# A pair's eight sums in two groups of four on four banks, and the row transposes behind the activations'

## The reference

```
for i in range(DEPTH):                       # 2 layers
    h = h + (gated_deltanet(...) if i == 0 else dilated_attention(...))
    h = h + hierarchical_moe(rms_norm(h), ...)
    h = h + per_layer_embedding(h, p[i], ...)
# hierarchical_moe: of 32 experts, each row goes to the best two of its best group
hdn = silu(xb @ w1[e]) * (xb @ w3[e])        # w1, w3: 1024 x 512
y   = hdn @ w2[e]                            # w2: 512 x 1024
out = zeros.at[row_tok].add(y * row_w)       # weighted rows summed back to their tokens
```

## Time and profile before

| | us |
|---|---|
| median of 3 runs | 1733.32 (1730.41 to 1734.15) |
| span of the profiled execution | 1731.8 |
| TensorE (PE) busy | 1677.2, 97% |
| VectorE (DVE) busy | 710.0, 41% |
| ScalarE (ACT) busy | 452.4, 26% |
| up products, L2158, 2040 matmuls | 460.7 |
| down products, L2195, 1008 matmuls | 223.4 |
| spread, L2145, 240 high and 240 low matmuls | 106.7 and 95.2 |
| adds, L2094, 240 | 154.0 |

### The profile page before, as it was taken

One profiled execution on the slowest core, in us unless ns is written; L12 is line 12 of the kernel. 1 busy time (PEld: TensorE's weight loads), 2 busy tenths in 40 slices (PEclk: granted clock), 3 DMA queues, 4 the chain that ended last, 5 costly groups with the idle time before them and its releaser, 6 DMA issues. The chain is left out here.

```text
span 1731.8 us, 20065 instructions
## 1 busy us (share of the span) xinstructions
PE 1677.2 (97%) x7380; PEld 806.9 (47%) x7380; DVE 710.0 (41%) x1514; ACT 452.4 (26%) x693; POOL 140.0 (8%) x192
## 2 busy tenths in 40 slices
PE   7999999998999999998999999998999999999898
PEld 4555566644334344343355564554343443434343
DVE  4778455515334343342333113365243443434241
ACT  5767233313010010101034716653110101101020
POOL 0026620001000000000000101100000000000000
PEclk9999999999999999999999999999999999999999
DMA  8121432286999999999991010058999999999950
GB/s 289 52 73 38 130 86 73 99 349 227 408 427 427 426 427 425 427 428 427 422 345 49 1 74 32 1 199 320 366 427 427 427 425 427 427 427 428 427 195 38
DMA packets 89355, 481.59 MB, mean 278 GB/s; under 512 B 22721, under 2 KB 39873, under 8 KB 62657
## 3 DMA queue, kind: packets, MB, share of 16 engines
q1 hardware_dynamic: 84672, 472.16, 67.3%
q0 software_dynamic: 4608, 8.40, 1.3%
HBM read 476.86 MB, written 12.06 MB: 282 GB/s over the span
## 5 line engine op out<-in xcount | busy, mean ns | idle before, releaser
L2158 PE MATMUL bank<-ring,xT 128*64 128x512 f32 x2040 | 460.7, 598 | 17.3 <-DMA ring<-in_w 16.4
L2094 DVE TENSOR_TENSOR H<-H,bank 128x512 f32<-128x512 f32 x240 | 154.0, 683 | 295.8 <-PE bank L2145 295.8
L2158 PEld LDWEIGHTS bank<-ring,xT 128*64 128x64 f32 x2040 | 140.1, 137 | 280.9 <-issue 264.8
L2195 PE MATMUL bank<-ring,sg 128*64 128x512 f32 x1008 | 223.4, 595 | 1.7 <-issue 1.2
L2195 PEld LDWEIGHTS bank<-ring,sg 128*64 128x64 f32 x1008 | 70.4, 137 | 131.0 <-issue 125.1
L705 PE MATMUL bank<-ring,ring 128*128 128x512 f32 x256 | 130.0, 604 | 0.0
L690 PE MATMUL bank<-ring,ring 128*128 128x512 f32 x256 | 112.9, 593 | 0.0
L2651 PE MATMUL bank<-ring,ring 128*128 128x512 f32 x256 | 110.5, 592 | 0.0
L2248 ACT ACTIVATE sg<-bank 128x512 f32<-128x512 f32 x32 | 19.2, 599 | 348.1 <-PE bank L2169 348.1
L2145 PE MATMUL bank<-high,Sb 128*128 128x512 f32 x240 | 106.7, 445 | 0.0
L2084 DVE SCALAR_TENSOR_TENSOR low<-bank,weight_now,high 128x512 fp32r<-128x512 f32 x60 | 45.1, 751 | 135.5 <-ACT high L2259 132.5
(11 more groups left out here) (346 smaller groups left out, 1985.1 us busy)
## 6 DMA issues: line engine op xcount, KB each, us to landing
ring<-in_w SPq DMA_DIRECT2D x178, 2048.0 KB, 28.6
ring<-in_w_heads SPq DMA_DIRECT2D x16, 1024.0 KB, 5.4
ring<-in_w SPq DMA_DIRECT2D x10, 1024.0 KB, 9.3
ring<-in_w SPq DMA_DIRECT2D x18, 512.0 KB, 7.4
ring<-in_w_ple_gate SPq DMA_DIRECT2D x4, 2048.0 KB, 28.7
ring<-in_w SPq DMA_DIRECT2D x4, 1536.0 KB, 8.2
ring<-in_w_kv SPq DMA_DIRECT2D x3, 2048.0 KB, 20.4
ring<-in_b_w_q SPq DMA_DIRECT2D x3, 2048.0 KB, 19.4
```

The costliest lines, as they stand in the source:

```text
L2094: dve.tensor_tensor(out, out, k.bank[6 + j % 2][:, :], ALU.add).then_inc(s.added, 1)
L2158: last = pe.matmul(out[e * SLOTS:(e + 1) * SLOTS, :], k.xT[:, at, e * SLOTS:(e + 1) * SLOTS], rows, start=(at == 0), stop=(at == DC - 1))
L2195: last = pe.matmul(k.bank[2 + n][e * SLOTS:(e + 1) * SLOTS, :], k.hT[:, c, e * SLOTS:(e + 1) * SLOTS], w[:, e, :], start=(c == 0), stop=(c ...
```

## The change

The sums of a pair are done in two groups. The first four stand where the first two stood, after the second half of `w1`; the second four after the second half of `w3`. They use banks 6, 7, 2, 3 and then 2, 3, 6, 7. Banks 2 and 3 are those of the down product, so the first group waits for both halves of the split, and the down product waits until the sums on banks 2 and 3 have been added. The activations' transposes come right behind the second group, and both halves of the next rows' transposes come behind these. VectorE adds the second four sums in one row, and evacuates both halves of the rows after them. The loop for more than 64 rows keeps banks 6 and 7.

```diff
+def spread_bank(j):
+    return (6, 7, 2, 3, 2, 3, 6, 7)[j]
-def add_results(dve, k, s, i, js):
+def add_results(dve, k, s, i, js, alone=False):
...
-        dve.tensor_tensor(out, out, k.bank[6 + j % 2][:, :], ALU.add).then_inc(s.added, 1)
+        bank = 6 + j % 2 if alone else spread_bank(j)
+        dve.tensor_tensor(out, out, k.bank[bank][:, :], ALU.add).then_inc(s.added, 1)
...
+def spread_matmuls(pe, k, s, j, bank):
+    n, t = j // NT, j % NT
+    for m, part in enumerate(parts_of(k, n)):
+        last = pe.matmul(bank[:, :], k.Sb[:, t * P:(t + 1) * P], part, start=(m == 0), stop=(m == 1))
+    last.then_inc(s.spread, 1)
+def spread_first(pe, k, s, i):
+    pe.wait_ge(s.Sb, i + 1)
+    pe.wait_ge(s.low, 2 * i + 2)
+    wait(pe, s.added, 8 * i)
+    for j in range(NT):
+        spread_matmuls(pe, k, s, j, k.bank[spread_bank(j)])
+def spread_second(pe, k, s, i):
+    for j in range(NT, 2 * NT):
+        if j < NT + 2:
+            pe.wait_ge(s.added, 8 * i + j - 1)
+        spread_matmuls(pe, k, s, j, k.bank[spread_bank(j)])
...
 def expert_down(pe, k, s, i, memory, arrived, alone=False, first=False):
     pe.wait_ge(s.hT, i + 1)
-    if not alone:
+    if not (alone or first):
         wait(pe, s.low, 2 * i)
+        pe.wait_ge(s.added, 8 * i - 2)
...
     pe.wait_ge(s.low, 2 * (PAIRS - 1))
+    pe.wait_ge(s.added, 8 * (PAIRS - 1) - 2)
...
-            spread(pe, k, s, i - 1, (0, 1))
+            spread_first(pe, k, s, i - 1)
         expert_up(pe, k, 1, 0, memory, k.bank[1], s.half2, arrived)
-        if not first:
-            spread(pe, k, s, i - 1, (2, 3))
         expert_up(pe, k, 1, 1, memory, k.bank[1], s.h3, arrived, apart=k.early_quarter if first else None)
         if not first:
-            spread(pe, k, s, i - 1, (4, 5))
+            spread_second(pe, k, s, i - 1)
+        expert_turn(pe, k, s, i)
         if not last:
             turn_rows(pe, k, s, i + 1, 0)
-        expert_turn(pe, k, s, i)
-        if not first:
-            spread(pe, k, s, i - 1, (6, 7))
-        if not last:
             turn_rows(pe, k, s, i + 1, 1)
...
         hidden(dve, k, s, i)
         if not first:
-            add_results(dve, k, s, i - 1, (4, 5))
+            add_results(dve, k, s, i - 1, range(NT, 2 * NT))
         if not last:
             evacuate_rows(dve, k, s, layer, i + 1, 0)
-        if not first:
-            add_results(dve, k, s, i - 1, (6, 7))
+            evacuate_rows(dve, k, s, layer, i + 1, 1)
         mark_tokens(dve, k, s, i, i)
-        if not last:
-            evacuate_rows(dve, k, s, layer, i + 1, 1)
```

More of the change, by code:

```diff
@@ L2132, in spread_last, with spread_alone @@
         last.then_inc(s.spread, 1)
[L2135 to L2146, removed]
+def spread_matmuls(pe, k, s, j, bank):
[14 more added lines that the diff above has]
+        spread_matmuls(pe, k, s, j, k.bank[spread_bank(j)])
+def spread_alone(pe, k, s, i):
+    pe.wait_ge(s.Sb, i + 1)
+    for j in range(2 * NT):
+        if j % NT == 0:
+            pe.wait_ge(s.low, 2 * i + j // NT + 1)
+        if j >= 2:
+            pe.wait_ge(s.added, 8 * i + j - 1)
+        spread_matmuls(pe, k, s, j, k.bank[6 + j % 2])
 def expert_up(pe, k, m, half, memory, out, done, arrived, each=None, apart=None):
@@ L2515, in more_tensor @@
     expert_down(pe, k, s, i - 1, memory, None, alone=True)
-    spread(pe, k, s, i - 1, range(NT), alone=True)
-    spread(pe, k, s, i - 1, range(NT, 2 * NT), alone=True)
+    spread_alone(pe, k, s, i - 1)
     identify_tokens(pe, k, s, pair, i, alone=True)
@@ L2532, in more_vector @@
     split_results(dve, k, s, i - 1)
-    add_results(dve, k, s, i - 1, range(2 * NT))
+    add_results(dve, k, s, i - 1, range(2 * NT), alone=True)
     dve.wait_ge(s.shift, i)
```

## The result

The changed kernel takes 1740.66 us, the median of ten runs (1736.70 to 1744.23), against 1733.91 for ten runs of the kernel before (1730.41 to 1738.26): a ratio of 1.0041 [1.0031, 1.0051]. The forecast was 1733.1 with a range up to 1736.0, so the time lies outside it, on the slower side. The profiled execution has a span of 1735.0 us and took 1736.76, one of the two shortest of the ten; its span is 3.2 us above that of before. In the changed kernel line L2158 is L2186, L2195 is L2224 and L2169 is L2197.

A forecast was written before the change was run, and what follows sets the result against it. TensorE was taken to bound the expert stage's first pairs, then the weight transfers. Profiled span 1731.8 + 0 (steady pairs) + 0 (first pairs) - 0.2 (last pairs) + 1.5 (median above span) = 1733.1 us; range 1729.5 to 1736.

The forecast's parts named there:

- What bounds the kernel: Expert stage: TensorE bounds the first pairs, then the weight transfers, at 29.4 us a pair against TensorE's 27.19.
- The groups, the transposes, VectorE and the waits added: Steady pair: groups save 0.20 and 0.09 us, transposes still cover the evacuation, VectorE and waits cost nothing; 0.29 us shorter.
- What becomes of the time saved: Steady pairs: at most 8.1 us saved, costed at zero; waits for the ring grow from 16.4 to about 24 us.
- Rival A: Steady pairs: the time saved is kept, up to 8.1 us faster, 1725.2, or half of it, 1729; chance 0.08.
- D: Every pair: evacuation or clear bank late, period stays 27.2 us, time unchanged at 1733, ring waits 16 us; chance 0.10.
- The first pair: First pair of a layer: down product 0 to 0.12 us later, but TensorE waits for the ring anyway, so 0.
- The last pair of a layer: Down product 6.89 us after the fourth piece's product starts, 0.08 less; two layers -0.2 us, between -0.5 and +0.9.
- Rival B: Last pair: a lengthened wait of 1.8 us drops TensorE's clock, 3.4 us slower, 1736.5, or twice that, 1739.9; chance 0.05.
- Rival C: Last pair uncovered: the branch comes behind the evacuation, +0.9 us, 1734.2; sign: down product over 8 us behind; chance 0.05.

The follow-up runs named there:

- e5: The changed kernel with 77 instructions put into layer 0's jumped-over loop, never executed; 1733.44 us, ratio 0.9997 to the kernel before.
- e8: e5 with half of two weight pieces left unloaded for pairs 5 to 15 of layer 1; 1716.23 us, 0.9902 of the kernel before.
- e7: The kernel before with half of two weight pieces left unloaded for pairs 5 to 15 of layer 1; 1723.70 us, ratio 0.9945.
- e6: The kernel before with 179 instructions put into layer 0's jumped-over loop, never executed; 1748.32 us, ratio 1.0094.

## Why the prediction was wrong

*What bounds the kernel.* Right. TensorE leads, then the transfers set the end; e5 against before (0.9997 [0.9987, 1.0007]) is a change of TensorE's work that the time doesn't see, and e8 against e7 the same change where it does.

*The groups, the transposes, VectorE and the waits added.* Right in the main: 2.04 and 1.95 for the groups, evacuation covered, no wait of TensorE for an add in a steady pair. The pair became 0.40 us shorter and not 0.29, mostly since the second matrix in one run saves another 0.14, which the sum left out; the transposes give 0.09 back. It had no consequence.

*What becomes of the time saved.* Right: zero, with the ring's waits at 25.1 us for a forecast of about 24. Rival A is refuted by e5, and D by the period of 26.79.

*The first pair.* The zero taken for it was not tested by itself; e5's time leaves no room for more than its interval, some 1.7 us either way.

*The last pair of a layer.* This is the step that failed. It took the branch at the 0.53 us of "issue" that the earlier trace rows show, and asked only what lies beside it: 6.89 us, or 7.42 if uncovered. Layer 0 came out at 6.86. In layer 1 the branch took 6.13 us, the product started 11.60 behind its piece, and half a clock then cost 1.93 more. The 0.53 was read as a property of the instruction. It is a property of where the instruction lies in the code, and the change had removed 76 instructions ahead of it. The term for the last pairs was bounded by -0.5 and +0.9 us for the two layers, from rows which all had the code in place; they measured +6.3 together, +6.56 in layer 1 and -0.2 in layer 0 (7.08 before, 6.86 after).

*Rival B* named a mechanism that did act, a clock that falls after TensorE has stood still, but for a wait of 1.8 us for the ring. Waits of up to 1.7 us came, and in the late pairs the clock stayed at 1.00; it fell during the stall of 5.39. *Rival C* had the right pair and the right instruction, and named 8 us as the sign that the forecast is wrong. Its price of 0.45 a layer was a tenth of what the place could cost.

## What to carry to other kernels

A kernel that branches can have a cost that no line of it shows: any edit that adds or removes instructions shifts the code behind it, and a jump may then land in code that is still to be fetched. When a change is slower with every engine's work as planned, look at the longest "issue" wait, then at the branch ahead of it, and set the loads of instructions against it in time; then put instructions into a branch that isn't taken and see whether the loss moves. In a kernel that branches, a gain or loss of a few microseconds by a rewrite may be the layout's and not the rewrite's.

## What the runs showed of the hardware

- TensorE's branch over 301 to 480 instructions takes 0.34 to 0.47 us in the table's rows when its target is there, against 0.05 us on ScalarE, and 6.13 to 6.23 us when it isn't, both beside DMA engines at a share of about 1.00. What the long one would cost beside idle DMA queues no run shows.
- In and behind such a stall the granted clock was 0.50 for 6.80 us, in the changed kernel and in both layers of e6; so a long branch cost some 7 us (6.75 for one, 14.9 for two) and not the 5 of the stall alone.
- A semaphore increment on TensorE's queue took about 0.16 us at the kernel's start: 12.6 us for 77 of them, 28.1 for 179.
- A DMA share of 1.00 does not say that the transfers are the bound. In e8, from 1250 to 1600 us, TensorE never waits and the share is still 1.00:

```profile
1250.00:1600.00 350.00, 350.00 (x1724) 150.81 (x1722) 135.86 (x314) 33.68 (x53) 12.86 (x13) 1.00 1.00 414
```
